# Modulation blocks in pairs: one bank, one evacuation and one folding for two blocks, adding transposes for the experts' sums, and another order of the blocks

## The reference, cut to what matters

```python
sh1, sc1, g1, sh2, sc2, g2 = split(silu(cvec) @ w_mod + b_mod, 6)  # w_mod is 1024 x 6144; one cvec per group of tokens
h = rms_norm(x, norm1_g) * (1 + sc1) + sh1
z = h @ w_in                                     # inputs of four parallel mixers
merged = sum(sigmoid(h @ w_mgate) * (y_mixer @ w_branch))
x = x + g1 * (merged @ w_out)
h2 = rms_norm(x, norm2_g) * (1 + sc2) + sh2
x = x + g2 * (routed_experts(h2) + shared_expert(h2))   # 32 experts, 4 for each token
```

## Time and profile before

| | |
|---|---|
| median of three runs | 1770.18 us |
| profiled execution: time, span | 1766.58 us, 1764.8 us |
| granted TensorE clock, mean | 0.967 of full |
| TensorE matmuls busy | 1619.8 us, 92% |
| VectorE, ScalarE, GpSimd busy | 29%, 24%, 12% |
| DMA, mean over the span | 219 GB/s |
| loads of `w_mod` | 24 of 2048 KB |
| loads of `acc` and `acc_second`, each layer | 3 and 3 of 512 KB |
| block matmuls (`ab<-slot,scT`) | 384 records: 16 for a block |
| folding matmuls (of `mod_rows` and `uT`) | 192 records: 8 for a folding |

### The profile page before, as it was taken

The page is one execution under the profiler, slowest core; times in us unless marked ns, Lnnn a source line. Parts: engine busy times, 40 slices in busy tenths (PEclk is TensorE's granted clock), DMA queues, the critical chain, the costliest instruction groups (busy, mean ns, idle before and its releaser), DMA issues. The chain is left out here.

```text
span 1764.8 us, 26274 instructions
## 1 busy us (share of the span) xinstructions
PE 1619.8 (92%) x9008; PEld 1016.0 (58%) x9008; DVE 518.8 (29%) x1309; ACT 429.1 (24%) x943; POOL 219.9 (12%) x182
## 2 busy tenths in 40 slices
PE   6999989999999997898889999899999998878887
PEld 3665556655676554455466656566558655555555
DVE  2055654411124111111141556542111431111113
ACT  3144224510122111111132342353001311111110
POOL 0003200000002133232100022000000022232220
PEclk8999999999998999999999999899999899999999
DMA  9512234452336999999982024326132299999993
GB/s 360 205 58 96 64 136 160 160 173 96 143 117 255 335 382 390 359 365 394 347 323 88 25 96 99 117 83 204 48 143 96 102 358 361 389 370 360 386 369 128
DMA packets 166113, 385.82 MB, mean 219 GB/s; under 512 B 21020, under 2 KB 58908, under 8 KB 165536
## 3 DMA queue, kind: packets, MB, share of 16 engines
q1 hardware_dynamic: 140976, 340.28, 52.1%
q0 software_dynamic: 16992, 24.96, 5.8%
q10 hardware_dynamic: 8016, 18.90, 2.9%
HBM read 372.27 MB, written 31.98 MB: 229 GB/s over the span
## 5 line engine op out<-in xcount | busy, mean ns | idle before, releaser
L786 PE MATMUL ab<-hT,slot 128*128 128x384 f32 x1344 | 452.8, 492 | 10.5 <-PEq L814 6.3
L786 PEld LDWEIGHTS ab<-hT,slot 128*128 128x128 f32 x1344 | 256.1, 192 | 194.3 <-issue 26.3
L786 PE MATMUL vb<-slot,arena 128*64 128x256 f32 x2560 | 307.2, 395 | 62.9 <-PEq L836 62.8
L786 PEld LDWEIGHTS vb<-slot,arena 128*64 128x64 f32 x2560 | 205.1, 142 | 147.9 <-issue 84.3
L688 POOL DMA_INDIRECT expert_sums<-arena,sum_index x72 | 112.9, 1568 | 362.2 <-POOLq L687 178.9
L2096 DVE SCALAR_TENSOR_TENSOR arena<-vb,unit_gate,arena 128x128 f32<-128x128 f32 x80 | 28.1, 351 | 386.4 <-DVEq L2095 386.4
L786 PE MATMUL ab<-slot,hT 128*128 128x384 f32 (+1 forms) x384 | 118.1, 463 | 0.0
L1540 ACT ACTIVATE arena<-vb 128x128 f32<-128x128 f32 x92 | 25.5, 278 | 362.0 <-ACTq L1539 362.0
L786 PE MATMUL vb<-nat,arena 128*64 128x512 f32 (+1 forms) x480 | 109.5, 535 | 1.8 <-PEq L954 1.2
L820 PEld LDWEIGHTS ab<-con,arena 128*128 128x128 f32 x532 | 60.2, 145 | 80.4 <-issue 79.1
L1411 ACT ACTIVATE con<-ab,sm 128x384 f32<-128x384 f32 x64 | 37.3, 582 | 277.2 <-ACTq L1309 277.1
(11 more groups left out here) (269 smaller groups left out, 1519.7 us busy)
## 6 DMA issues: line engine op xcount, KB each, us to landing
slot<-in_w_up SPq DMA_DIRECT2D x64, 2048.0 KB
slot<-in_w_mod SPq DMA_DIRECT2D x24, 2048.0 KB
slot<-in_w_mgate SPq DMA_DIRECT2D x32, 1024.0 KB
nat<-in_w_down SPq DMA_DIRECT2D x32, 1024.0 KB, 18.2
slot<-in_w_in SPq DMA_DIRECT2D x10, 2048.0 KB
arena<-in_w_down SPq DMA_DIRECT2D x16, 1024.0 KB, 19.3
hT<-in_w_down SPq DMA_DIRECT2D x16, 1024.0 KB, 20.1
slot<-in_w_out SPq DMA_DIRECT2D x4, 2048.0 KB
```

The source lines that it names most:

```text
L786: i = nc.tensor.matmul(out, lhsT, rhs, start=start, stop=stop, skip_group_check=True)
```

## The change

The 12 blocks of a layer become 6 pairs; pair k is blocks 2k and 2k+1, one sixth of the modulation. Both blocks of a pair go into one bank: `scT` has 34 columns with the two vectors in columns 2 and 3; the first block reads columns 2 to 33 and fills rows 0 and 1 of each strip, the second reads columns 0 to 31 and adds into rows 2 and 3. One evacuation, one folding (4 matmuls with 4 columns) and one addition of the bias follow for a pair. Where the blocks stand:

| | before, blocks | after, pairs (blocks) |
|---|---|---|
| start | 4 | 2 (4) |
| attention of layer 0 | 7 | 4 (8) |
| gap of layer 0 | 3 | 1 (2) |
| end of layer 0 | 2 | 0 |
| first norm of layer 1 | 2 | 1 (2) |
| attention of layer 1 | 4 | 3 (6) |
| gap of layer 1 | 2 | 1 (2) |

```diff
-START_MODS = [(0, b) for b in (2, 3, 0, 1)]
-ATT_MODS = [[(0, b) for b in range(4, 11)], [(1, b) for b in range(6, 10)]]
-GAP_MODS = [[(0, 11), (1, 2), (1, 3)], [(1, 10), (1, 11)]]
-TAIL_MODS = [(1, 0), (1, 1)]
-NORM_MODS = [(1, 4), (1, 5)]
+START_MODS = [(0, 1), (0, 0)]
+ATT_MODS = [[(0, 2), (0, 3), (0, 4), (0, 5)], [(1, 2), (1, 3), (1, 4)]]
+GAP_MODS = [(1, 1), (1, 5)]
+TAIL_MOD = (1, 0)
...
-    plan = (("6m7", "8m9", "amb", "cmd", "mem", "mf"),
-            ("6m7", "89", "ab", "cd", "mem", "mf"))[l]
+    plan = (("6m7", "89", "amb", "cd", "em", "mf"),
+            ("6m7", "89", "ab", "cd", "em", "mf"))[l]
...
-            unit(x) if kind == "unit" else passing(1)
+            unit(x) if kind == "unit" else passing(2)
...
@@ SP
                 if l == 0:
                     mods(START_MODS)
                 else:
-                    mods(TAIL_MODS)
+                    lm, k = TAIL_MOD
+                    columns("w_mod", 2 * k, l=lm)
                     sums_back()
-                    mods(NORM_MODS)
+                    columns("w_mod", 2 * k + 1, l=lm)
...
@@ TensorE
                 def mod_block():
-                    s, w = slot()
                     def block(o):
-                        for c in range(KC):
-                            q = 32 * (c % 4)
-                            last = mm(o[q:q + 32, :], scT[:, c, :], wview(w)[:, c, :], c < 4, c >= 4, c == KC - 1)
+                        for half in range(2):
+                            s, w = slot()
+                            for c in range(KC):
+                                q = 32 * (c % 4)
+                                last = mm(o[q:q + 32, :], scT[:, c, 2 - 2 * half:34 - 2 * half], wview(w)[:, c, :],
+                                          half == 0 and c < 4, half == 1 and c >= 4, half == 1 and c == KC - 1)
+                            release.append(freed[s])
                         return last
                     group(a, block)
-                    release.append(freed[s])
...
                 else:
-                    for _ in NORM_MODS:
-                        mod_block()
-                    for k in range(len(NORM_MODS)):
-                        mod_turned(mod_pair[k])
+                    mod_block()
+                    mod_turned()
...
                 if l == 0:
                     sl.restart(SLOTS[1])
-                    mod_block()
...
                 last_pair_down()
-                if l == 0:
-                    mod_block()
-                    mod_turned(mod_pair[0])
                 flush()
                 pe.wait_ge(last_rows_ready, 1).then_inc(last_rows_ready, -1)
-                sums = [(v, v.next()) for _ in range(4)] + [(a, a.next()) for _ in range(4)]
+                sums = [(a, a.next()) for _ in range(4)] + [(v, v.next()) for _ in range(4)]
...
-                for c, (ring, b) in enumerate(sums):
-                    bank, full = (vb[b], vfull[b]) if ring is v else (ab[b], afull[b])
-                    for t in range(NT):
-                        if c == 0:
-                            pe.wait_ge(acc_added, 1).then_inc(acc_added, -1)
-                        last = mm(bank[:, P * t:P * t + P], acc[:, t, c:D:KC], ident, False, t == NT - 1)
-                    last.then_inc(full, 1)
-                if l == 0:
-                    mod_turned(mod_pair[1])
+                for t in range(NT):
+                    pe.wait_ge(acc_added, 1).then_inc(acc_added, -1)
+                    for c, (ring, b) in enumerate(sums):
+                        bank, full = (vb[b], vfull[b]) if ring is v else (ab[b], afull[b])
+                        last = nc.tensor.matmul(bank[:, P * t:P * t + P], acc[:, t, c:D:KC], ident, start=False,
+                                                stop=t == NT - 1, is_transpose=True, skip_group_check=True)
+                        if t == NT - 1:
+                            last.then_inc(full, 1)
...
@@ VectorE, end of a layer
-                if l == 0:
-                    modulated(*TAIL_MODS[0])
...
+                for c in range(KC):
+                    if c < KC // 2:
+                        b = spare.next()
+                        bank, full = ab[b], afull[b]
+                    else:
+                        b = v.next()
+                        bank, full = vb[b], vfull[b]
+                    dve.wait_ge(full, 1).then_inc(full, -1)
+                    vec.scalar_tensor_tensor(xT[:, c, 0:P], bank[:, 0:P], mT[:, l, 5, c, 0:1], xT[:, c, 0:P],
+                                             ALU.mult, ALU.add)
+                    vec.scalar_tensor_tensor(xT[:, c, P:T], bank[:, P:T], mT[:, l, 5, c, 1:2], xT[:, c, P:T],
+                                             ALU.mult, ALU.add).then_inc(x_ready, 1)
+                settle()
+                for b in range(NBANK):
+                    dve.sem_inc(afree[b], 1)
+                    dve.sem_inc(vfree[b], 1)
```

More of the change, by code:

```diff
@@ L579, in mods @@
                 def mods(which):
-                    for lm, b in which:
-                        columns("w_mod", b, l=lm)
+                    for lm, k in which:
+                        for half in range(2):
+                            columns("w_mod", 2 * k + half, l=lm)
                 if l == 0:
@@ L887, in fold @@
                         for n in range(4):
-                            last = mm(o[:, 2 * n:2 * n + 2], rows[:, P * n:P * n + P], c_("fold")[:, 0:2], True, True, True)
+                            last = mm(o[:, 4 * n:4 * n + 4], rows[:, P * n:P * n + P], c_("fold")[:, 0:4], True, True, True)
                         return last
@@ L1115, in _ @@
                 mean_square()
-                for _ in range(2):
-                    mod_block()
-                mod_turned(mod_pair[0])
-                for _ in GAP_MODS[l][2:]:
-                    mod_block()
-                mod_turned(mod_pair[1])
+                mod_block()
+                mod_turned()
                 def router(o):
@@ L1376, in _ @@
                 else:
+                    mod_row()
                     warm(ACT.Sigmoid)
-                    for k in range(len(NORM_MODS)):
-                        mod_row(mod_pair[k])
                 act.wait_ge(shift_known, 1).then_inc(shift_known, -1)
@@ L1517, in _ @@
                 warm(ACT.Sigmoid)
-                for k in range(2):
-                    mod_row(mod_pair[k])
-                held = [a.next() for _ in GAP_MODS[l][2:]]
+                mod_row()
                 shift(1)
@@ L1656, in _, with modulated @@
                     settle()
-                def modulated(lm, b):
+                def modulated(lm, k):
                     def add(o):
[L1660 to L1663, removed]
+                        bias = bm[:, lm, 16 * k:16 * k + 16].rearrange("p (y n x) -> p y n x", y=2, n=4)
+                        return vec.tensor_tensor(mT[:, lm, k, :, :].rearrange("p (y n) x -> p y n x", y=2),
+                                                 o[:, 0:16].rearrange("p (n y x) -> p y n x", y=2, x=2), bias, ALU.add)
                     empty(add)
@@ L1946, in _, with residual @@
                 scales(1)
-                def residual(s, take=empty):
+                def residual(s):
                     for c in range(KC):
@@ L1955, in add @@
                                                             ALU.mult, ALU.add)
-                        take(add)
+                        empty(add)
                         tell(x_ready)
@@ L2152, in _ @@
                 spare = Cursor(range(NBANK))
[L2153 to L2158, removed]
-                    if c < KC // 2:
[L2160 to L2167, removed]
+                for c in range(KC):
+                    if c < KC // 2:
+                        b = spare.next()
[12 more added lines that the diff above has]
+                    dve.sem_inc(vfree[b], 1)
             tell(y_ready)
```

36 lines of the change are left out of this document (7 added, 29 removed).

## The result

| | before | after |
|---|---|---|
| median, lowest to highest (20 runs each) | 1770.2 us, 1763.05 to 1774.77 | 1774.16 us, 1768.01 to 1777.72 |
| ratio, 95% interval | 1 | 1.0024, 1.0013 to 1.0034 |
| profiled execution: time, span | 1766.58, 1764.8 us | 1776.78, 1773.9 us |
| TensorE matmuls busy | 1619.8 us, 9008 records | 1594.8 us, 8864 records |

The change makes the kernel 4.0 us slower: a small loss, where a gain of 1.2 us within the noise was forecast. TensorE has 25 us less work and the kernel takes longer, so it waits more.

What follows compares the result with a forecast made beforehand. TensorE bounds the attention, a chain between engines the stretch from experts to norm. Terms -0.8 + 2.8 + 14.3 - 12.8 - 1.8 - 2.3 - 0.6 gave -1.2 us, 1769.0 on the median; range 1759 to 1777.

Steps and rivals of the forecast that it cites:

- blocks and foldings in the attention: TensorE's own work: layer 0 one block more, three foldings fewer, -0.8 us; layer 1 two more, one fewer, +2.8.
- halves of the last pair wait, both layers: End of each attention: TensorE waits 2.2 us for the first half's load and 3.5 for the second's, 11.4 in all.
- low clock behind them: Attention, behind the waits for the halves: matmuls at 1.2 GHz cost 0 to 5 us a layer, 2.5 taken.
- first gate of the second pass: Behind the attention: its earlier waits of 1.5 and 0.6 us vanish because its load is there, -2.1 us.
- end of layer 1, with the output's issue: Eight channels at 0.72 us end at 1756.8, not 1759.0; drain and semaphore increments cost 0.4: -1.8 us.
- start: Kernel's beginning: last half starts about 30.2 when its weights are in, projection at 38.3, not 40.62: -2.3 us.
- gap of layer 0: VectorE takes the scores without queuing behind the third block's bias: -0.6 us.
- The ring: Attention's weight slots: pairs "em" and "mf" share two slots, so reloads of 8.3 us make TensorE wait 5.7 us a layer.
- The boundary: Layer 0's experts to layer 1's norm: earlier one-hot matmuls, single-record transposes, faster VectorE channels, -12.8 us.
- Rival 2: Layer 1's mean square runs at 1.2 GHz after TensorE's waits and transposes, +5.8 us: 1774.8 us; chance 0.15.
- rival 3: VectorE's residual keeps its 1.43 us a channel at both layer ends, +11.4 us: 1780.2 us; chance 0.05.
- sign of being wrong: Either TensorE does not wait for slots, or layer 0's experts to layer 1's norm give back less than 10 us.

Runs made afterwards that it cites:

- experiment 1: Changed kernel with its modulation pairs set apart, two or more units between pairs and before the second pass; 1754.56 us, ratio 0.9917 to the kernel before.
- experiment 6: Changed kernel with only each layer's last pair moved, from the attention's last step to unit 8; 1754.22 us, ratio 0.9926 to the kernel before.
- experiment 2: Changed kernel with the next mean square's bank given back with the residual's second channel, not behind the last; 1766.26 us, ratio 0.9990 to the kernel before.
- experiment 3: Kernel before, with only the expert sums turned by TensorE's transpose mode in place of a product with the identity; 1762.3 us, ratio 0.9962 to before.

## Why the prediction was wrong

The terms of its sum against the two traces, in us:

| term | forecast | measured |
|---|---|---|
| blocks and foldings in the attention | -0.8 + 2.8 = +2.0 | -0.8 + 2.6 = +1.8, what is left of the stretches below |
| halves of the last pair wait, both layers | +11.4 | 3.73 + 2.08 + 3.52 + 1.70 = +11.0 |
| low clock behind them | +5.0 | +1.3 + 1.7 in layer 0, +3.4 in layer 1 = +6.4 |
| **first gate of the second pass** | **-2.1** | **+2.1 + 2.35 = +4.4** |
| layer 0's experts to layer 1's projection | -12.8 | 37.3 - 48.0 = -10.7 |
| end of layer 1, with the output's issue | -1.8 | -4.8 + 0.7 = -4.1 |
| start | -2.3 | 38.27 - 40.62 = -2.35 |
| gap of layer 0, from its mean square to the experts' tables | -0.6 | (568.69 - 522.87) - (560.50 - 513.41) = -1.3, of it -0.75 at VectorE's first use of the scores |
| `w_out` and layer 1's first projection at lower clock | not in it | +3.3 + 1.1 = +4.4 |

The measured terms come to +9.6, the spans differ by 9.1. (Not in the table: from `w_out` to ScalarE's copy the changed kernel is 0.6 and 0.9 us faster in the two layers, and from the output's issue to the end 0.9 slower.) The first term is each layer's attention, projections included, less the waits and clock of the next three rows: in layer 0 -2.35 at the start became +7.75 behind the first gate, 10.1 less 10.9; in layer 1 -3.08 became +11.60, 14.7 less 11.0 and the projection's 1.1.

- **The step that failed** is "In return the gate behind the attention ... will find it loaded, since TensorE comes later". It has the sign wrong: -2.1 us became +4.4, 6.5 us over both layers. The slots were played through for the two pairs and not one place further: branch and gate of the second pass come next in the list and take x and y again. The branch's load can start only when x is given free, which happens with the first matmul of the late second half, and the gate's load stands behind it: 13.5 and 13.7 us from the branch's issue to the gate. Experiments 1 and 6 show it: with the last pair elsewhere all these waits are gone, and 19 and 17 us with them. The forecast priced the whole matter at 14.3, the traces at 21.8. By my estimate a drain behind the first half would give x free 2 us earlier; no run tests it. The gate's 0.57 us of the earlier trace rows were never the slot: they stand in experiments 1 and 6 too, with the load in time, so by my estimate at most 1.52 - 0.57 = 0.95 us, in layer 0, could have been gained.
- **The ring itself** was right in mechanism and place: 5.8 and 5.2 us of waits against 5.7. That the sum came out is in part luck. From the end of the first half to the next user of its slot it took 9.8 and 9.6 us (337.54 to 347.36, 1206.63 to 1216.20), not 8.3: the 8.3 end with the last data, and TensorE started some 1.1 us behind that (data until about 351.5, the half at 352.68). So the first wait was 3.7 and 3.5 us and not 2.2, and the second 2.1 and 1.7 and not 3.5, because the first half, at the lower clock, took 1.3 and 1.7 us longer and covered as much of it.
- **The boundary** was forecast 2.1 us too good, by two errors that nearly cancel. A strided transpose takes 0.11 us and not 0.249, and the one-hot matmuls started 5.8 us behind ScalarE's copy and not 7.3, so the residual ended 19.6 us behind it and not 23.1. The reason given for 0.249, that reading with a stride is slow, does not hold for a transpose. (The same transposes made the end of layer 1 better by 2.3 us than forecast.) And the mean square was taken to follow the squares, while its bank was held until all eight channels were done: 5.6 us lost with the clock (experiment 2). The diff shows it, eight increments behind a drain; I priced them for the output (0.4) and did not ask who waits for the banks. Rival 2 saw the mean square at the lower clock, for another reason, and its 1774.8 us is nearly the time measured; that is luck, since the bank's loss was balanced and the gate's was not in it.
- **VectorE's pitch** (rival 3) did fall, to 0.65 us. The Trainium skill (VectorE: DVE Perf Modes, The DRAIN you can't avoid) says that the pipeline is emptied after every operation anyway and that a semaphore costs nothing extra. That is no ground for the channels to keep their 1.43: what the change leaves out is an explicit drain instruction, which is another thing, and the emptying itself no run here tests. The same two operations take 0.99 us a channel with it and its semaphore (experiment 3) and 0.65 without. Still my reading of the earlier trace rows, "most of it the drain and the wait", missed that 0.44 of the 1.43 was TensorE's. (Rival 3's time, by its own terms, is 1769.0 + 11.4 = 1780.4, not 1780.2.)
- **`w_out`** is no effect of the change that these runs show. Its 128 records in layer 0, before and after:

```profile
471.93 41.65 PE L786 MATMUL vb<-merged,slot 128*128 128x384 f32 x128 [2.08 <-PEq L795]
```

```profile
479.69 43.34 PE L785 MATMUL vb<-merged,slot 128*128 128x384 f32 x128 [2.08 <-PEq L794]
```

The wait ahead is the same, the granted clock over the next 10 us is 1.00 in the one and 0.83 in the other, and the experiments have both lengths within one kernel (43.34 and 41.64 in experiment 1, 41.64 and 43.21 in experiment 2, 43.34 twice in 3). In both layers together (1.7 and 1.6 us) that is 3.3 of the 9.1 us between the two profiled spans; it is the likely reason why the medians lie closer, but which of the two comes how often outside profiled executions was not measured.

On the medians the forecast's -1.2 us became +4.0. The gate's 6.5 us are more than the whole of that 5.2, and the bank's 5.6 us were roughly paid for by the cheap transposes. Neither sign of being wrong that the prediction named came up: TensorE waits for slots, and the boundary gives back 10.7 us; none of them looked at the gate.

## What to carry to other kernels

When a list of buffers is played, play it until every slot has been reused once by work of another kind: what suffers is also the first load behind the changed stretch, and its place in the queue adds to its wait. A release that rides on the engine's next instruction is as late as that instruction: here it waited for a load itself. When a change bundles the release of several buffers to save a drain, ask for each who takes it next; a release can ride on the next operation of the same engine, and cost VectorE nothing here (0.65 us a channel in both). And a pitch of two engines in step says nothing about either alone: take one's work away before you credit the other.

## What was unexpected of the hardware

- In transpose mode a float32 block of 128 x 128, read from `acc` with a stride of 8 elements, takes 0.11 us, the same as a contiguous one (0.12 from the earlier trace rows); as a product with the identity it takes two records of 0.24 to 0.25.
- At equal length of wait (2.08 us) the clock behind it differs between the profiled executions (one for each kernel) and even between the two layers of one: 41.65 or 43.3 us for the same 128 records.
